# Where the high and low parts of a weight tile lie: two tensors, or one with the two parts value by value in turn

## The chip, the cores and the metric

The kernel runs on one core of a Trainium2 chip. The time is the device time of one execution in microseconds (us), from the first to the last of what the device does for it. The core has a matrix engine (TensorE, in the rows PE for the matmuls and PEld for the loads of the operand that is held in the array), a vector engine (VectorE, DVE), a scalar engine (ScalarE, ACT), a general engine (GpSimd, POOL) and a queue engine (SyncE, SP) that issues most DMAs. Each has its own list of instructions; they wait for one another by semaphores. Data lie in an on-chip memory of 128 partitions; matmul results go to eight banks of an accumulator memory.

## The reference

A stack of two layers on 256 tokens of width 1024, in float32. Each layer has a mixer (six mLSTM heads, five neighbourhood attention heads, five GLA heads in both directions), a cross-attention into 256 memory tokens, and a gated feed-forward block with a depthwise convolution. What matters here are the large products with weights:

```python
proj = h @ w_in                       # 1024 x 3512, cut into 13 parts
mixed @ w_out                         # 1024 x 1024
q = h @ wq; k = mem_n @ wk; v = mem_n @ wv; o @ wo
u = h @ w_up                          # 1024 x 5632
a, g = u[..., :D_FF], u[..., D_FF:]
a = dwconv_centred(a, conv_w, conv_b)
(jax.nn.gelu(a) * g) @ w_down         # 2816 x 1024
```

## The kernel before, in words

**Products in three passes.** A float32 matrix is split into a high part, which is the value rounded to the matmul's narrower format (float32r), and a low part, the rest. A product W x is then W_hi x_hi + W_hi x_lo + W_lo x_hi, all added up in one bank.

**Units.** The weights come in 144 units of at most 1 MB (128 partitions by up to 2048 float32), in the order that `UNITS` lists. Three slots (`RING` = 3) hold them. For each unit:
- SyncE issues the load into `raw` (line 573), once VectorE is done with the unit that was in that slot three before.
- ScalarE copies raw to the high part, `whi` (line 1108, in `hi_upto`), once the data have landed and the matmuls of the unit three before are done.
- VectorE writes raw minus high to the low part, `wlo` (line 1462, in `lo_upto`).
- TensorE waits for that (`have`) and runs the unit's matmuls, taking its operands from `weights`.

**Two kinds of unit.** In a feature-major unit (made by `fm`, with `KT` = 8 blocks of 128 input features, up to 256 output columns) the weights are the operand that is held in the array, 128 by 128 at a time, and the tokens stream through. They are used in `fm_blocks` (for each block three matmuls of 256 columns, the high weights against the high and the low tokens and the low weights against the high: lines 685 to 687 with a token tile xhi, xlo, chi or clo as the moving operand) and in `fm_joint` (line 723: high weights against the high and low tokens together, 512 columns; line 724: low weights against the high tokens, 256 columns). The gate and up projections of the FFN, the queries and keys of the cross-attention and nine units of each input projection are of this kind: 78 of 144. In the others (made by `tm`, 4 blocks, and the FFN's down projection, 2 blocks) a token tile is held, and the weights stream through as the moving operand, in up to 512 columns.

In the rows, `bank<-xhi,whi` names first the moving operand and then the held one.

**What sets the order.** Each engine's list is written out by hand; ScalarE and VectorE run the splits of later units between other work, at the places where `split_hi` and `split_lo` stand. In the FFN a group `p` uses three units: fa (gate), fg (up) and the down unit of the group before.

Of the kernel before, what the change touches and what calls it, by code (L numbers as in the profile page):

```python
# [15 lines left out]
F32R = mybir.dt.float32r  # L16
ALU = mybir.AluOpType
ACT = mybir.ActivationFunctionType
# [3 lines left out]
P = 128  # L22
# [4 lines left out]
TT, KT = T // P, DM // P  # L27
# [18 lines left out]
def layer_units(l):  # L46

    u = []

    def fm(name, m, *columns, at=l):  # L50
        u.append(((at, name), m, 0, KT, columns))

    def tm(name, m, c, n, halves="ab"):
        for half in halves:
            u.append(((l, name + half), m, 4 * "ab".index(half), 4, ((c, n),)))

    fm("gq", "w_in", (C_GQ, P))
    fm("mix", "w_in", (C_G, 32), (C_GQ + P, 32), (C_GK + P, 32), (C_GA, 32))
    fm("qk0", "w_in", (0, 256))
    fm("nqk4", "w_in", (C_NQ + 256, DH), (C_NK + 256, DH))  # L60
    fm("qk1", "w_in", (256, 256))
    fm("qk2", "w_in", (512, 256))
    tm("v", "w_in", C_V, ML)
    fm("nq", "w_in", (C_NQ, 256))
    fm("nk", "w_in", (C_NK, 256))
    fm("gk", "w_in", (C_GK, P))
    tm("nv", "w_in", C_NV, NA)
    tm("gv", "w_in", C_GV, GV)
    tm("o", "w_in", C_O, ML)
    tm("gg", "w_in", C_GG, GV)  # L70
    for i in range(2 if l else 0, 4):
        fm(f"xk{i}", "w_xk", (256 * i, 256))
    tm("xv0", "w_xv", 0, 512)
    tm("xv1", "w_xv", 512, 512, "a")
    tm("wo0", "w_out", 0, 512)
    tm("wo1", "w_out", 512, 512)
    tm("xv1", "w_xv", 512, 512, "b")
    for i in range(4):
        fm(f"xq{i}", "w_xq", (256 * i, 256))
    tm("xw0", "w_xo", 0, 512)  # L80
    tm("xw1", "w_xo", 512, 512)
    if l + 1 < DEPTH:
        fm("xk0", "w_xk", (0, 256), at=l + 1)
    for p in range(NP):
        fm(f"fa{p}", "w_up", (256 * p, 256))
        fm(f"fg{p}", "w_up", (FF + 256 * p, 256))
        if p:
            u.append(((l, f"fd{p - 1}"), "w_down", 2 * p - 2, 2, ((0, DM),)))
    u.append(((l, f"fd{NP - 1}"), "w_down", 2 * NP - 2, 2, ((0, DM),)))
    if l + 1 < DEPTH:  # L90
        fm("xk1", "w_xk", (256, 256), at=l + 1)
    return u

UNITS = [u for l in range(DEPTH) for u in layer_units(l)]
# [3 lines left out]
SIZE = [nk * w for (_, _, _, nk, _), w in zip(UNITS, WCOLS)]  # L98
RING = 3
UW = 2048  # L100
# [198 lines left out]
def build(nc, a, out):  # L299
    with ExitStack() as ctx:  # L300
        def sb(name, shape, dt=F32):
            return ctx.enter_context(nc.sbuf_tensor(name, shape, dt))

        def sem(name):
            return ctx.enter_context(nc.semaphore(name))
# [1 line left out]

        sb("to_line", [P, LINE // 4 - 48])
        raw = sb("raw", [P, RING, UW])
        whi = sb("whi", [P, RING, UW], F32R)  # L310
        wlo = sb("wlo", [P, RING, UW], F32R)

        h = sb("h", [P, TT, DM])
        tmb = sb("tmb", [P, TT, DM])
# [62 lines left out]
        rt = sb("rt", [P, TT])  # L377
        eps = sb("eps", [P, 1])
        gbias = sb("gbias", [24, 1])
        used = [0]  # L380

        def carve(*shape, at=None):
# [68 lines left out]
        hi_done = sem("hi_done")  # L451
        lo_done = sem("lo_done")
# [73 lines left out]
        def is_used(eng, l, unit):  # L526
            eng.wait_ge(te_done, USED[l, unit])
# [140 lines left out]
        def _(pe):  # L668
# [3 lines left out]
            for l in range(DEPTH):  # L672
# [15 lines left out]

                def weights(key, nk):
                    gu = UNIT[key]  # L690
                    return tuple(w[:, gu % RING, 0:SIZE[gu]].rearrange("p (k n) -> p k n", k=nk) for w in (whi, wlo))

                def fm_blocks(name, group, blocks, fresh=False, at=l):

                    u = at, name
                    if blocks[0][:2] == (0, 0):
                        free(name, at)
                    have(u)
                    hi, lo = weights(u, KT)
                    x = PAIR[group]  # L700
                    for f, k0, k1 in blocks:
                        for k in range(k0, k1):
                            if fresh and f == 0:
                                lo_is(pe, l, group, k)
                            cs = slice(f * P, f * P + P)
                            last = split_mm(bank_of(at, name, 2, T)[:, f, :], hi[:, k, cs], lo[:, k, cs], x[0][:, k, :], x[1][:, k, :],
                                            k == 0 and (f == 0 or k1 == KT), k == KT - 1)
                    if blocks[-1][2] == KT and blocks[-1][0] == WCOLS[UNIT[u]] // P - 1:
                        last.then_inc(te_done, 1)

                def fm_joint(name, fresh):

                    u = l, name
                    have(u)
                    hi, lo = weights(u, KT)
                    for f in range(2):
                        free(f"{name}{f}")
                        o = bank(f"{name}{f}")
                        for k in range(KT):
                            if fresh and f == 0:  # L720
                                lo_is(pe, l, "n2" if name[:2] == "xq" else "n3", k)
                            cs = slice(f * P, f * P + P)
                            mm(o, hi[:, k, cs], ypair[:, k].rearrange("p a n -> p (a n)"), start=k == 0, stop=False, skip_group_check=True)  # L723
                            last = mm(o[:, 0:T], lo[:, k, cs], yhi[:, k, :], start=False, stop=k == KT - 1, skip_group_check=True)  # L724
                        last.then_inc(te_done, 1)
# [4 lines left out]
                def tm_half(unit, half, names, n, group, fresh=False, tokens=(0, 1), ks=range(4)):  # L730
                    have((l, unit + half))
                    hi, lo = weights((l, unit + half), 4)
                    x = PAIR[group]
                    for t in tokens:
                        if half == "a":
                            free(names[t])
                        for k in ks:
                            kk = 4 * "ab".index(half) + k
                            if fresh and t == 0:
                                lo_is(pe, l, group, kk)  # L740
                            s = slice(t * P, t * P + P)
                            last = split_mm(bank(names[t])[:, 0:n], x[0][:, kk, s], x[1][:, kk, s],
                                            hi[:, k, :], lo[:, k, :], kk == 0, kk == KT - 1)
                        if (half == "b" or t == TT - 1) and k == 3:
                            last.then_inc(te_done, 1)
# [76 lines left out]
                if l == 0:  # L822
                    pe.wait_ge(memn_ready, TT)
                    for i in range(4):
                        free(f"mt_{i}")
                        for kk in range(2):
                            for t in range(TT):
                                k = 2 * i + kk
# [12 lines left out]
                for hh in range(MLH + 1):  # L841
# [7 lines left out]
                    if hh:  # L849
# [3 lines left out]
                        w = PT[:, g % 2, :]  # L853
# [194 lines left out]
                for p in range(NP + 1):  # L1048
# [3 lines left out]
                    if p:  # L1052
# [4 lines left out]
                        hi, lo = weights(u, 2)  # L1057
                        for i in (0, 2, 1, 3):
                            n, t = i // 2, i % 2
# [12 lines left out]
        def _(act):  # L1072
            A = nc.scalar.activation
# [28 lines left out]
            def hi_upto(l, unit):  # L1102
                while nhi[0] <= UNIT[l, unit]:
                    gu = nhi[0]
                    act.wait_ge(landed[gu % RING], 16 * LANDS[gu])
                    if gu >= RING:
                        is_used(act, *UNITS[gu - RING][0])
                    A(whi[:, gu % RING, 0:SIZE[gu]], raw[:, gu % RING, 0:SIZE[gu]], ACT.Copy).then_inc(hi_done, 1)  # L1108
                    nhi[0] += 1

            act.wait_ge(const_ready, 1)
# [6 lines left out]
            for l in range(DEPTH):  # L1118
# [5 lines left out]
                def split_hi(unit):  # L1124
                    hi_upto(l, unit)
# [250 lines left out]
                if l + 1 < DEPTH:  # L1376
                    hi_upto(l + 1, "xk0")
# [30 lines left out]
                if l + 1 < DEPTH:  # L1408
                    hi_upto(l + 1, "xk1")
# [14 lines left out]
        def _(dve):  # L1424
            V = nc.vector
            ts, tt, stt = V.tensor_scalar, V.tensor_tensor, V.scalar_tensor_tensor
# [30 lines left out]
            def lo_upto(l, unit):  # L1457
                while nlo[0] <= UNIT[l, unit]:
                    gu = nlo[0]
                    dve.wait_ge(hi_done, gu + 1)  # L1460
                    n_ = SIZE[gu]
                    tt(wlo[:, gu % RING, 0:n_], raw[:, gu % RING, 0:n_], whi[:, gu % RING, 0:n_], ALU.subtract).then_inc(lo_done, 1)  # L1462
                    nlo[0] += 1

            for l in range(DEPTH):
# [5 lines left out]
                def split_lo(unit):  # L1471
                    lo_upto(l, unit)
# [92 lines left out]
                for hh in range(MLH):  # L1565
                    is_filled(dve, l, f"mlb{hh}")
                    nb = bank(f"mlb{hh}", 2, T)
                    e, w = E[:, hh % 2, :], PT[:, hh % 2, :]
# [201 lines left out]
                if l + 1 < DEPTH:  # L1770
                    lo_upto(l + 1, "xk0")
# [32 lines left out]
                if l + 1 < DEPTH:  # L1804
                    lo_upto(l + 1, "gq")
# [4 lines left out]
                for i in (0, 2, 1, 3):  # L1810
                    n, t = i // 2, i % 2
# [46 lines left out]
```

## Time and profile before

| | us |
|---|---|
| median of three runs (lowest, highest) | 899.81 (896.81, 899.89) |
| the profiled execution's own time | 897.88 |
| its span, first to last instruction | 896.0 |
| TensorE busy with matmuls | 876.3 |
| TensorE's weight loads, beside them | 771.3 |
| VectorE busy | 626.8 |
| ScalarE busy | 525.2 |
| mean granted TensorE clock | 0.996 |

Matmuls overlap in the array and their ends are modelled, so a single matmul's busy time is longer than the distance between two starts. The distance of starts is what a stream costs. The busy time of a weight load also holds a fixed part. Durations of VectorE and ScalarE are those of one instruction after another.

### The profile page before, as it was taken

How to read it: one execution, taken by the hardware profiler on the slowest of the kernel's cores; microseconds unless marked ns; L12 is line 12 of the kernel's file. 1: busy time of each engine (PE TensorE's matmuls, PEld its weight loads, DVE VectorE, ACT ScalarE, POOL GpSimd, SP SyncE). 2: the span in 40 equal slices, each digit the busy share in tenths (PEclk: the TensorE clock that was granted, in tenths of full speed). 3: DMA queues.
4: the chain of work that ended last, by engine and by line, in shares of the span. 5: the costliest groups of instructions: out<-in, count | busy, mean ns of one | idle time of the engine just before them, and what ended most of it. 6: DMA issues, size and time to landing. Idle time of an engine off the chain costs nothing.

```text
span 896.0 us, 13415 instructions
## 1 busy us (share of the span) xinstructions
PE 876.3 (98%) x5453; PEld 771.3 (86%) x5453; DVE 626.8 (70%) x915; ACT 525.2 (59%) x782; POOL 15.3 (2%) x37
## 2 busy tenths in 40 slices
PE   6999999999999999999999999999999899999997
PEld 5999998888888888888899999888888788888885
DVE  5787588758557767667667975877664677667665
ACT  6954673647547556556576546735645655555555
POOL 5000000000000000000000000000000000000000
PEclk9999999999999999999999999999999999999999
DMA  9745453265154655555558254425352356565541
GB/s 280 219 113 157 166 164 121 97 232 188 48 188 157 219 188 188 188 189 187 141 150 231 80 161 165 142 95 188 140 189 95 128 177 212 188 196 180 189 165 47
DMA packets 128680, 146.68 MB, mean 164 GB/s; under 512 B 23165, under 2 KB 109547, under 8 KB 128619
## 3 DMA queue, kind: packets, MB, share of 16 engines
q1 hardware_dynamic: 128404, 145.55, 50.5%
q8 instruction: 43, 0.70, 0.3%
q10 hardware_dynamic: 214, 0.28, 0.1%
q14 instruction: 19, 0.15, 0.0%
HBM read 144.77 MB, written 1.05 MB: 163 GB/s over the span
## 4 chain that ended last, share of the span: by engine, by line
PE 91%; DVE 4%; ACT 3%; issue 1%; DMA 1%; SPq 1%; POOL 0%; DVEq 0%; ACTq 0%; POOLq 0%
PE bank L723 21%; PE bank L685 15%; PE bank L687 15%; PE bank L686 15%; PE bank L724 11%; PE bank L758 2%; PE bank L859 2%; PE bank L1030 2%; PE bank L1017 2%; DVE wlo L1462 2%; ACT whi L1108 1%; PE bank L891 1%; PE bank L868 1%; PE bank L777 1%; DMA raw<-in_w_in 1%
## 5 line engine op out<-in xcount | busy, mean ns | idle before, releaser
L1462 DVE TENSOR_TENSOR wlo<-raw,whi 128x2048 fp32r<-128x2048 f32 (+3 forms) x144 | 306.1, 2134 | 93.5 <-ACT whi L1108 92.9
L723 PE MATMUL bank<-ypair,whi 128*128 128x512 f32 x832 | 294.9, 398 | 0.6 <-DVE ypair L1478 0.5
L1108 ACT ACTIVATE whi<-raw 128x2048 fp32r<-128x2048 f32 (+3 forms) x144 | 256.5, 1787 | 36.6 <-PE bank L687 28.9
L724 PE MATMUL bank<-ypair,wlo 128*128 128x256 f32 x832 | 233.4, 280 | 0.0
L723 PEld LDWEIGHTS bank<-ypair,whi 128*128 128x128 f32 x832 | 156.2, 188 | 40.4 <-DVE wlo L1462 1.4
L724 PEld LDWEIGHTS bank<-ypair,wlo 128*128 128x128 f32 x832 | 157.1, 189 | 0.8
L685 PE MATMUL bank<-xhi,whi 128*128 128x256 f32 x320 | 93.7, 293 | 1.1 <-DVE wlo L1462 0.9
L686 PE MATMUL bank<-xlo,whi 128*128 128x256 f32 x320 | 91.2, 285 | 0.0
L687 PE MATMUL bank<-xhi,wlo 128*128 128x256 f32 x320 | 91.2, 285 | 0.0
L685 PE MATMUL bank<-whi,xhi 128*128 128x512 f32 (+2 forms) x256 | 90.1, 352 | 0.0
L687 PE MATMUL bank<-whi,xlo 128*128 128x512 f32 (+2 forms) x256 | 88.5, 346 | 0.0
L686 PE MATMUL bank<-wlo,xhi 128*128 128x512 f32 (+2 forms) x256 | 88.4, 345 | 0.0
L685 PE MATMUL bank<-whi,fhi 128*128 128x512 f32 x176 | 69.1, 393 | 0.0
L687 PE MATMUL bank<-whi,flo 128*128 128x512 f32 x176 | 68.8, 391 | 0.0
L686 PE MATMUL bank<-wlo,fhi 128*128 128x512 f32 x176 | 68.6, 390 | 0.0
L685 PEld LDWEIGHTS bank<-xhi,whi 128*128 128x128 f32 x320 | 62.1, 194 | 5.7 <-issue 4.1
L686 PEld LDWEIGHTS bank<-xlo,whi 128*128 128x128 f32 x320 | 62.2, 194 | 0.0
L687 PEld LDWEIGHTS bank<-xhi,wlo 128*128 128x128 f32 x320 | 62.1, 194 | 0.0
L685 PEld LDWEIGHTS bank<-whi,xhi 128*128 128x128 f32 x256 | 48.1, 188 | 5.1 <-issue 1.3
L687 PEld LDWEIGHTS bank<-whi,xlo 128*128 128x128 f32 x256 | 48.1, 188 | 3.8
L686 PEld LDWEIGHTS bank<-wlo,xhi 128*128 128x128 f32 x256 | 48.1, 188 | 3.5
L1392 ACT ACTIVATE arena<-bank 128x256 f32<-128x256 f32 x44 | 16.3, 380 | 57.4 <-PE bank L724 57.4
(264 smaller groups left out, 1194.0 us busy)
## 6 DMA issues: line engine op xcount, KB each, us to landing
raw<-in_w_up SPq DMA_DIRECT2D x44, 1024.0 KB, 5.0
raw<-in_w_down SPq DMA_DIRECT2D x22, 1024.0 KB, 5.0
raw<-in_w_in SPq DMA_DIRECT2D x10, 1024.0 KB, 6.2
raw<-in_w_xk SPq DMA_DIRECT2D x8, 1024.0 KB, 4.8
raw<-in_w_xv SPq DMA_DIRECT2D x8, 1024.0 KB, 4.9
raw<-in_w_out SPq DMA_DIRECT2D x8, 1024.0 KB, 4.9
raw<-in_w_xq SPq DMA_DIRECT2D x8, 1024.0 KB, 5.6
raw<-in_w_xo SPq DMA_DIRECT2D x8, 1024.0 KB, 5.0
```

Source lines behind the costliest of these rows:

```text
L685: mm(o, s_hi, m_hi, start=first, stop=False, skip_group_check=True)
L686: mm(o, s_hi, m_lo, start=False, stop=False, skip_group_check=True)
L687: return mm(o, s_lo, m_hi, start=False, stop=last, skip_group_check=True)
L723: mm(o, hi[:, k, cs], ypair[:, k].rearrange("p a n -> p (a n)"), start=k == 0, stop=False, skip_group_check=True)
L724: last = mm(o[:, 0:T], lo[:, k, cs], yhi[:, k, :], start=False, stop=k == KT - 1, skip_group_check=True)
L758: last = mm(bank(names[t])[:, 0:n], x[:, k, t * P:(t + 1) * P], w[:, k, :], start=k + i == 0, stop=False, skip_group_check=True)
L859: last = mm(o[:, t, d, :], w[:, c:c + P], mv[:, jt, g, :], start=i == 0, stop=i == len(src) - 1)
L1017: last = mm(bank(f"xs{hh}", TT, T)[:, t, :], xq[:, 2 * hh + kk, t * P:(t + 1) * P], xk[:, 2 * hh + kk, :], start=kk == 0, stop=kk == 1)
L1030: last = mm(bank(f"xo_{hh}", 2, T)[:, f, :], xv[:, jt, hh * XD + f * P:hh * XD + (f + 1) * P], xpt[:, hh, jt, :], start=jt == 0, stop=jt == 1)
L1108: A(whi[:, gu % RING, 0:SIZE[gu]], raw[:, gu % RING, 0:SIZE[gu]], ACT.Copy).then_inc(hi_done, 1)
L1392: A(fx[:, f, :], bank(f"fa{p}{f}")[:, T:2 * T], ACT.Copy).then_inc(fa_copied, 1)
L1462: tt(wlo[:, gu % RING, 0:n_], raw[:, gu % RING, 0:n_], whi[:, gu % RING, 0:n_], ALU.subtract).then_inc(lo_done, 1)
```

## The change

The tensors `whi` and `wlo`, each 128 partitions by 3 slots by 2048, become one tensor `whl`, 128 by 3 by 4096: as many bytes, in the same place. A new helper, `parts`, gives the two parts of a unit. For a feature-major unit (8 blocks) the slot holds high and low values in turn, high value 0, low value 0, high value 1, low value 1, and so on, and each part is a view with a step of two values, which is 8 bytes. For the other units the high part is the first half of the slot and the low part begins at its middle; each is contiguous, as before. ScalarE's copy, VectorE's subtraction and TensorE's operands take these views. `raw`, the transfers, the semaphores and the order of instructions on every engine are the same.

```diff
-        whi = sb("whi", [P, RING, UW], F32R)
-        wlo = sb("wlo", [P, RING, UW], F32R)
+        whl = sb("whl", [P, RING, 2 * UW], F32R)
...
+        def parts(gu):
+
+            w, n = whl[:, gu % RING, :], SIZE[gu]
+            if UNITS[gu][3] == KT:
+                v = w[:, 0:2 * n].rearrange("p (n a) -> p a n", a=2)
+                return v[:, 0, :], v[:, 1, :]
+            return w[:, 0:n], w[:, UW:UW + n]
+
...
                 def weights(key, nk):
                     gu = UNIT[key]
-                    return tuple(w[:, gu % RING, 0:SIZE[gu]].rearrange("p (k n) -> p k n", k=nk) for w in (whi, wlo))
+                    return tuple(w.rearrange("p (k n) -> p k n", k=nk) for w in parts(gu))
...
-                    A(whi[:, gu % RING, 0:SIZE[gu]], raw[:, gu % RING, 0:SIZE[gu]], ACT.Copy).then_inc(hi_done, 1)
+                    A(parts(gu)[0], raw[:, gu % RING, 0:SIZE[gu]], ACT.Copy).then_inc(hi_done, 1)
...
-                    n_ = SIZE[gu]
-                    tt(wlo[:, gu % RING, 0:n_], raw[:, gu % RING, 0:n_], whi[:, gu % RING, 0:n_], ALU.subtract).then_inc(lo_done, 1)
+                    hi, lo = parts(gu)
+                    tt(lo, raw[:, gu % RING, 0:SIZE[gu]], hi, ALU.subtract).then_inc(lo_done, 1)
```

## Rows read from the trace of the kernel before

**Rows 1.** Busy time of each engine, from the page.
```profile
PE 876.3 (98%) x5453; PEld 771.3 (86%) x5453; DVE 626.8 (70%) x915; ACT 525.2 (59%) x782; POOL 15.3 (2%) x37
```

**Rows 2.** The chain that ended last, from the page: share by engine.
```profile
PE 91%; DVE 4%; ACT 3%; issue 1%; DMA 1%; SPq 1%; POOL 0%; DVEq 0%; ACTq 0%; POOLq 0%
```

**Rows 3.** Costliest groups: line, engine, out<-in, count | busy, mean ns | idle before.
```profile
L723 PE MATMUL bank<-ypair,whi 128*128 128x512 f32 x832 | 294.9, 398 | 0.6 <-DVE ypair L1478 0.5
...
L724 PE MATMUL bank<-ypair,wlo 128*128 128x256 f32 x832 | 233.4, 280 | 0.0
L723 PEld LDWEIGHTS bank<-ypair,whi 128*128 128x128 f32 x832 | 156.2, 188 | 40.4 <-DVE wlo L1462 1.4
...
L685 PE MATMUL bank<-xhi,whi 128*128 128x256 f32 x320 | 93.7, 293 | 1.1 <-DVE wlo L1462 0.9
...
L685 PEld LDWEIGHTS bank<-xhi,whi 128*128 128x128 f32 x320 | 62.1, 194 | 5.7 <-issue 4.1
```

**Rows 4.** Timeline of TensorE in a 256-column stream: start us, duration us, instruction.
```profile
502.30 0.28 PE L686 MATMUL bank<-xlo,whi 128*128 128x256 f32 x1
...
503.01 0.28 PE L686 MATMUL bank<-xlo,whi 128*128 128x256 f32 x1
```

**Rows 5.** Timeline of TensorE in a joint stream of the FFN.
```profile
364.66 0.40 PE L723 MATMUL bank<-ypair,whi 128*128 128x512 f32 x1
364.90 0.28 PE L724 MATMUL bank<-ypair,wlo 128*128 128x256 f32 x1
365.02 0.40 PE L723 MATMUL bank<-ypair,whi 128*128 128x512 f32 x1
...
367.84 0.40 PE L723 MATMUL bank<-ypair,whi 128*128 128x512 f32 x1
```

**Rows 6.** Timeline of the weight loads, after a wait.
```profile
710.37 0.19 PEld L723 LDWEIGHTS bank<-ypair,whi 128*128 128x128 f32 x1 [0.31 <-DVE wlo L1462]
710.48 0.19 PEld L724 LDWEIGHTS bank<-ypair,wlo 128*128 128x128 f32 x1
```

**Rows 7.** Groups of instructions by form: the two splits, 2048 values.
```profile
L1462 DVE TENSOR_TENSOR wlo<-raw,whi 128x2048 fp32r<-128x2048 f32 x116 | 265.0, 2290 | 89.7 <-ACT whi L1108 89.3
...
L1108 ACT ACTIVATE whi<-raw 128x2048 fp32r<-128x2048 f32 x116 | 221.2, 1911 | 34.0 <-PE bank L687 28.9 <-PE bank L758 4.5 <-DMA raw<-in_w_in 0.4
```

**Rows 8.** Single lines: min/median/max ns, first and last start us, forms.
```profile
L1646 DVE SCALAR_TENSOR_TENSOR den<-arena x2: 194/194/195, 106.8 to 554.6; 128x24 f32<-128x24 f32 x2
...
L1590 DVE SCALAR_TENSOR_TENSOR arena<-arena,tmb x2: 1218/1218/1218, 59.2 to 507.7; 128x1024 f32<-128x1024 f32 x2
...
L1711 DVE SCALAR_TENSOR_TENSOR gg<-eg,gg x2: 817/819/821, 159.7 to 598.0; 128x640 f32<-128x640 f32 x2
```

**Rows 9.** Busy time by engine in one group of the FFN: window, length, us.
```profile
358.40:375.20 16.80, 16.80 (x90) 14.32 (x89) 11.55 (x14) 9.31 (x11) 0.00 (x0) 1.00 0.57 188
```

**Rows 10.** Timeline of VectorE in the FFN.
```profile
362.82 2.29 DVE L1462 TENSOR_TENSOR wlo<-raw,whi 128x2048 fp32r<-128x2048 f32 x1 [1.11 <-ACT whi L1108]
```

**Rows 11.** Timeline of TensorE where the next unit's stream begins.
```profile
369.61 0.40 PE L723 MATMUL bank<-ypair,whi 128*128 128x512 f32 x1
```

**Rows 12.** The chain in order of time, where the splits stand in it.
```profile
14.51 1.92 ACT whi L1108
16.46 2.30 DVE wlo L1462
...
202.71 1.81 ACT whi L1108
204.54 2.30 DVE wlo L1462
...
554.74 1.81 ACT whi L1108
556.64 2.29 DVE wlo L1462
...
641.09 1.81 ACT whi L1108
642.92 2.30 DVE wlo L1462
```

**Rows 13.** Timeline of TensorE in another joint stream.
```profile
721.92 0.39 PE L723 MATMUL bank<-ypair,whi 128*128 128x512 f32 x1
...
723.31 0.39 PE L723 MATMUL bank<-ypair,whi 128*128 128x512 f32 x1
```

## The prediction

> **What bounds the kernel now.** I read the busy times first. TensorE is busy for 876.3 of 896.0 us, its weight loads for 771.3 us beside that, VectorE for 626.8 and ScalarE for 525.2 us [rows 1]. The chain of waits says the same: 91% of the span runs over TensorE, 4% over VectorE, 3% over ScalarE [rows 2]. So a change counts in two ways only: it alters the pace of the matmul stream, or it makes one of the few waits for weights longer. The costliest groups come next [rows 3]. The matmuls that hold a weight tile in the array are L723 and L724 (832 of each) and the L685, L686 and L687 that stream xhi or xlo (320 of each, and 32 of each with chi and clo). These have their stationary operand, a 128x128 piece of whi or wlo, loaded once for every matmul. The others stream whi and wlo and hold a token tile; their units keep the old layout.
>
> Busy times of single matmuls say little about pace, since they overlap. I take the pace from starts in the timeline. In a stream of 256-column matmuls, starts are 0.118 us apart (502.30 to 503.01, six steps) [rows 4]. In the joint stream of L723 (512 columns) and L724 (256), nine pairs take 3.18 us (364.66 to 367.84), 0.353 us a pair; of a pair, 0.24 us go by under the 512 columns and 0.11 to 0.12 us under the 256 [rows 5]. How fast a weight load can follow another is seen where the array was empty: after a wait, two loads start at 710.37 and 710.48, 0.11 us apart [rows 6]. So under a 256-column matmul the load fits with some 0.01 us to spare, and under a 512-column one with more than 0.1 us.
>
> **The change, part by part.** No instruction, wait, transfer or semaphore is added, removed or moved; three kinds of operand get a step.
>
> (a) Weight loads, 2 x 832 + 3 x 352 = 2720 of them, read 128 values with a step of 8 bytes instead of 4. The trace has no load with that step, so I bound it. Now a load walks through 512 bytes of a partition in 0.11 us, 4.7 bytes per ns. With the step it walks through 1024. If it goes on at 4.7 bytes per ns, it takes 0.22 us; if only the count of values matters, 0.11 us as now; less than now is possible only if the load were not paced by its 128 values, for which no row speaks. The nearest row is the moving operand of the same engine: L723's 512 columns are 2048 bytes, walked in 0.24 us at most [rows 5], 8.5 bytes per ns or more. At that pace the 1024 bytes take 0.12 us at the most. I take 0.11 us: cost nothing. The cover is thin: every ns by which a load outgrows the slot costs 832 + 1056 = 1888 ns, 1.9 us, because the loads that lie under 256 columns are those for L723 (832) and those for the 1056 short matmuls. The 832 loads for L724 lie under 512 columns.
>
> The Trainium skill (SBUF — State Buffer, Door 1, the box on cachelines) says that the memory has lines of 16 bytes and that two accesses to a line are enough for full bandwidth. A step of 8 bytes gives just two, so by that rule the sum is that of no change. No row of this case shows a line.
>
> (b) ScalarE's copy that writes the high part (L1108), 1.91 us for 2048 values, and (c) VectorE's subtraction that reads it and writes the low part (L1462), 2.29 us [rows 7]. Of the 144 units, 78 are of the changed kind (70 of them with 2048 values). The nearest row for a step on VectorE is L1646, which reads two operands of 24 values with a step of 260 bytes: 194 ns. The same kind of instruction without a step is L1590, 1218 ns for 1024 values, and L1711, 819 for 640 [rows 8]: (1218 - 819) / 384 = 1.04 ns a value and 153 ns fixed, so 24 values would be 178 ns. The step of 260 bytes cost 16 ns, 0.7 ns a value. For a step of 8 bytes that is the upper end, 1.4 us for 2048 values; the lower is zero. I know no row for a step in ScalarE's writes; I give it the same two ends. I take zero for both, because 260 bytes puts each value far from the last and 8 bytes does not, but this is a guess between two ends and I keep the upper one as a rival.
>
> Even the upper end would mostly be hidden. A group of the FFN lasts 16.8 us, in which VectorE works 11.55 and ScalarE 9.31 us [rows 9]; two changed units add 2.9 us to each. The subtractions end long before their use: the one that ends at 365.11 (362.82 + 2.29) [rows 10] is for the weights whose stream begins at 369.61 [rows 11], 4.5 us later. The places with no cover are those where copy and subtraction stand in the chain of waits: four such pairs of changed units, at 14.51, 202.71, 554.74 and 641.09 us [rows 12]. There the cost would be 4 x 2 x 1.4 = 11 us.
>
> **The sum** against the profiled execution's own 897.9 us (span 896.0): 0 + 0 + 0. The median of the three runs is 899.8, 1.9 us above the profiled one, and the comparison is made with such runs, so the forecast is 900.
>
> **Rivals.** (A) The strided load is paced by bytes, not values. Slower: a load of 0.22 us and the 0.01 us by which a short slot now exceeds its load give 0.23 us where 0.118 stands. 1056 x 0.11 = 116 us in the L685 to L687 streams and 832 x 0.11 = 92 us in the joint ones: 897.9 + 208 = 1106 us. It decides from the point where a load needs more than the 0.118 us of a slot; a load of 0.123 us would already cost about 9 us. For it speaks that the margin is 0.01 us and that weight loads are the one stream that must cover twice the ground; against it, that the same engine already moves through memory at that pace for its other operand.
>
> (B) The step slows VectorE and ScalarE as 260 bytes did. TensorE keeps its pace, the hidden part stays hidden, and the four uncovered places cost 11 us: 911 us. For it: 16 ns of L1646. Against: the step there is over 32 times as long. The Trainium skill (Vector Engine (DVE) Microarchitecture Reference, 5.2 Measured stream behaviour on trn2) speaks for it: a port keeps its rate only with pairs of adjacent words, and values one by one cost 1.7 to 2.5 ns each. By its highest figure a subtraction would take 3 us more, and two of them in a group would lift VectorE to 17.5 of 16.8 us; it would then bind in the FFN. L1646 agrees in size (1.04 + 0.7 ns a value); the page has no figure for a step of 8 bytes.
>
> (C) The pace changes by itself. The joint stream knows two rhythms: 0.353 us a pair in rows 5, but four pairs in 1.39 us, 0.3475 a pair, elsewhere [rows 13], at the same granted clock and with the same instructions. If the new loads tipped all of it into the quicker one, 832 x 0.0058 = 4.8 us would go: 895 us. Nothing in the change points to it, and the slower rhythm is already the usual one, so it can hardly get worse by this.
>
> **Chances.** No change 0.65; A (in full or by some ns a load) 0.14; B 0.13; C 0.08. What a measurement of this kernel can tell from no change is about 0.5%, 4.5 us; the three runs lie within 3.1 us. Faster by more than that: C, 0.08, and 0.01 for what I did not think of. Slower: A and B together, 0.27. Within: 0.64. The range of 8 in 10 reaches down to C and up over B, 894 to 912; A in full is left out.
>
> **What would show it.** Right: starts in the 256-column streams 0.118 us apart, joint pairs at 0.3475 to 0.353 us, L1108 and L1462 at 1.91 and 2.29 us as a mean of the 2048 forms. A shows as short matmuls 0.13 to 0.23 us apart and weight loads longer than their 188 to 194 ns [rows 3], while the streams of whi and wlo keep their pace. B shows as L1462 of 2048 values above 2.3 us and L1108 above 1.9, and TensorE waits on L1462 at the four places. C shows as pairs at 0.3475 us throughout. I would be wrong if the load pays for its step by only a few ns, which no view of the old kernel can exclude.

## The result and the profile after

The changed kernel takes 902.13 us (median of 20 runs, 899.23 to 904.69), the kernel before 899.92 in the same measurement. The ratio is 1.0025, 95% interval 1.0014 to 1.0035. A repeat beside other kernels gave 1.0027 (1.0012 to 1.0041). So the step of 8 bytes costs about a quarter of a per cent, 2.2 us: less than the 0.5% that I called a change, but a real loss and not zero. Its profiled execution has a span of 899.9 us.

The page answers to [rows 1] with VectorE as it was, 2 us more of matmuls, 10 us more of ScalarE and 9 us more of weight loads:

```profile
PE 878.2 (98%) x5453; PEld 779.9 (87%) x5453; DVE 625.9 (70%) x915; ACT 535.6 (60%) x782; POOL 14.9 (2%) x37
```

Where they come from is in the groups by form (busy us, mean ns), which answer to [rows 3, 7]. The helpers moved the lines by seven: L1469 is the subtraction, L1115 the copy, L730 and L731 the joint stream.

```profile
L1469 DVE TENSOR_TENSOR whl<-raw,whl 128x2048 fp32r<-128x2048 f32 x116 | 265.1, 2291 | 94.9 <-ACT whl L1115 94.8
L1115 ACT ACTIVATE whl<-raw 128x2048 fp32r<-128x2048 f32 x116 | 233.4, 2017 | 29.9 <-PE bank L694 25.3 <-PE bank L765 4.4
L731 PEld LDWEIGHTS bank<-ypair,whl 128*128 128x128 f32 x832 | 163.7, 197 | 0.7
L730 PEld LDWEIGHTS bank<-ypair,whl 128*128 128x128 f32 x832 | 162.7, 196 | 34.4 <-DVE whl L1469 2.0 <-issue 0.7
```

The subtraction reads one operand and writes the other with the step, and costs nothing more: 2291 against 2290 ns. The copy went from 1911 to 2017 ns on the mean of 116. Only 70 of them are of the changed kind, and those went from 1911 to 2085 ns, 0.17 us more each. A weight load of the joint stream records 196 or 197 ns instead of 188.

Does the longer load slow the stream? The starts of TensorE, against [rows 4] and [rows 5]:

```profile
503.09 0.28 PE L693 MATMUL bank<-xlo,whl 128*128 128x256 f32 x1
...
503.81 0.28 PE L693 MATMUL bank<-xlo,whl 128*128 128x256 f32 x1
...
366.24 0.40 PE L730 MATMUL bank<-ypair,whl 128*128 128x512 f32 x1
...
369.42 0.40 PE L730 MATMUL bank<-ypair,whl 128*128 128x512 f32 x1
```

Six steps of the short stream take 0.72 us, 0.120 each, and nine joint pairs 3.18 us, 0.353 each. Taken over all such steps, the median of the short streams is 120 ns in both traces. The joint pairs go from 354.0 to 355.6 ns on the mean, which contains the longer waits, and from 350 to 354 on the median. The loads after a wait, where nothing else is in the array, answer to [rows 6]:

```profile
714.53 0.19 PEld L730 LDWEIGHTS bank<-ypair,whl 128*128 128x128 f32 x1 [0.45 <-DVE whl L1469]
714.64 0.20 PEld L731 LDWEIGHTS bank<-ypair,whl 128*128 128x128 f32 x1
```

To the nanosecond, such pairs of loads start 108 or 109 ns apart before and 114 to 117 ns apart now. The slot under a 256-column matmul is 120 ns. It just holds. And the wait itself, 0.31 us before [rows 6], is 0.45 us: this is where the change is paid.

Both traces have the same 5453 matmuls in the same order, so each step from one start to the next can be compared. There are exactly eight places at which the step is longer, by 0.14 us or more, in the changed kernel and stays so in every trace with strided copies, and not in the traces below with copies of the old length. With the start before and the growth: 111.65 us (0.15), 206.89 (0.18), 274.58 (0.17), 458.70 (0.25), 466.96 (0.18), 559.47 (0.16), 645.27 (0.18), 710.37 (0.16). Together 1.4 us. Two of the places, before and after:

```profile
206.88 0.19 PEld L723 LDWEIGHTS bank<-ypair,whi 128*128 128x128 f32 x1 [0.37 <-DVE wlo L1462]
458.69 0.86 PEld L777 LDWEIGHTS bank<-ident,tmb 128*128 128x128 f32 x8 [0.19 <-DVE tmb L1453]
```
```profile
207.30 0.19 PEld L730 LDWEIGHTS bank<-ypair,whl 128*128 128x128 f32 x1 [0.54 <-DVE whl L1469]
459.69 0.85 PEld L784 LDWEIGHTS bank<-ident,tmb 128*128 128x128 f32 x8 [0.44 <-DVE tmb L1460]
```

Four of the eight waits (206.89, 274.58, 645.27, 710.37) end with a subtraction. The one at 458.70 ends with `tmb`, a normalised tile that VectorE writes after a subtraction: the longer copy delays what stands behind it in the engines' lists too. For the other three the profile names no releaser. In the chain of the kernel before, five of the eight waits are not seen as such. They are put down as part of a matmul, as the one at 710.37, where the usual step is 0.24 us:

```profile
710.39 0.47 PE bank L723
```

The rest of the profiled difference of 3.9 us is TensorE's clock. In the windows (length, then busy us, then granted clock, DMA share, GB/s) the kernel before has a stretch at the lower level, 1.2 GHz, in the first and the changed one in the second:

```profile
476.00:484.00 8.00, 8.00 (x44) 6.99 (x43) 4.93 (x6) 6.62 (x9) 0.00 (x0) 0.79 0.73 149
584.00:592.00 8.00, 8.00 (x93) 6.53 (x88) 7.75 (x22) 0.52 (x1) 0.00 (x0) 1.00 0.35 109
```
```profile
476.00:484.00 8.00, 8.00 (x55) 6.80 (x54) 4.51 (x8) 5.58 (x8) 0.00 (x0) 1.00 0.77 182
584.00:592.00 8.00, 8.00 (x104) 6.29 (x101) 6.26 (x17) 1.20 (x1) 0.00 (x0) 0.57 0.23 69
```

From 575 to 600 us the changed kernel takes 3.1 us longer. Its gain near 480 us is 1.5 us, of which 0.8 goes to a longer wait that follows at 502 us. So 1.4 + 3.1 - 0.7 = 3.8 of the 3.9 us are accounted for.

### The profile page after: what moved, and what is told of

Same layout as the page of the kernel before. It is cut to its first block, busy times and chain, and to the rows that moved or that the text cites. A ratio compares the mean times of both kernels' runs of the same rounds, so it can differ in the third digit from the quotient of the medians.

```text
span 899.9 us, 13415 instructions
## 1 busy us (share of the span) xinstructions
PE 878.2 (98%) x5453; PEld 779.9 (87%) x5453; DVE 625.9 (70%) x915; ACT 535.6 (60%) x782; POOL 14.9 (2%) x37
## 3 DMA queue, kind: packets, MB, share of 16 engines
HBM read 144.77 MB, written 1.05 MB: 162 GB/s over the span
## 4 chain that ended last, share of the span: by engine, by line
PE 83%; DVE 7%; ACT 7%; issue 1%; DMA 0%; DVEq 0%; ACTq 0%
PE bank L730 20%; PE bank L692 13%; PE bank L693 13%; PE bank L694 13%; PE bank L731 10%; DVE whl L1469 3%; ACT whl L1115 3%; PE bank L765 2%; PE bank L866 2%; PE bank L1037 2%; PE bank L1024 2%; ACT ypair L1139 1%; PE bank L898 1%; PE bank L784 1%; DVE ypair L1727 1%
## 5 line engine op out<-in xcount | busy, mean ns | idle before, releaser
L1469 DVE TENSOR_TENSOR whl<-raw,whl 128x2048 fp32r<-128x2048 f32 (+3 forms) x144 | 306.2, 2135 | 99.0 <-ACT whl L1115 98.6
L730 PE MATMUL bank<-ypair,whl 128*128 128x512 f32 x832 | 295.4, 398 | 1.3 <-DVE whl L1469 0.6
L1115 ACT ACTIVATE whl<-raw 128x2048 fp32r<-128x2048 f32 (+3 forms) x144 | 269.4, 1877 | 32.5 <-PE bank L694 25.3
L731 PE MATMUL bank<-ypair,whl 128*128 128x256 f32 x832 | 232.8, 280 | 0.0
L730 PEld LDWEIGHTS bank<-ypair,whl 128*128 128x128 f32 x832 | 162.7, 196 | 34.4 <-DVE whl L1469 2.0
L731 PEld LDWEIGHTS bank<-ypair,whl 128*128 128x128 f32 x832 | 163.7, 197 | 0.7
L692 PE MATMUL bank<-xhi,whl 128*128 128x256 f32 x320 | 92.9, 290 | 2.3 <-DVE whl L1469 1.7
L692 PE MATMUL bank<-whl,xhi 128*128 128x512 f32 (+2 forms) x256 | 90.6, 354 | 0.0
L694 PE MATMUL bank<-xhi,whl 128*128 128x256 f32 x320 | 90.4, 283 | 0.0
L693 PE MATMUL bank<-whl,xhi 128*128 128x512 f32 (+2 forms) x256 | 88.7, 346 | 0.0
L693 PE MATMUL bank<-whl,fhi 128*128 128x512 f32 x176 | 68.7, 390 | 0.0
L692 PE MATMUL bank<-whl,fhi 128*128 128x512 f32 x176 | 68.7, 390 | 0.0
L692 PEld LDWEIGHTS bank<-xhi,whl 128*128 128x128 f32 x320 | 62.5, 195 | 6.9 <-issue 5.6
L694 PEld LDWEIGHTS bank<-xhi,whl 128*128 128x128 f32 x320 | 62.5, 195 | 0.0
L692 PEld LDWEIGHTS bank<-whl,xhi 128*128 128x128 f32 x256 | 48.3, 189 | 5.3 <-issue 1.5
L693 PEld LDWEIGHTS bank<-whl,xhi 128*128 128x128 f32 x256 | 48.4, 189 | 3.5
```

What stands on the lines that cost most here:

```text
L692: mm(o, s_hi, m_hi, start=first, stop=False, skip_group_check=True)
L693: mm(o, s_hi, m_lo, start=False, stop=False, skip_group_check=True)
L694: return mm(o, s_lo, m_hi, start=False, stop=last, skip_group_check=True)
L1115: A(parts(gu)[0], raw[:, gu % RING, 0:SIZE[gu]], ACT.Copy).then_inc(hi_done, 1)
L1469: tt(lo, raw[:, gu % RING, 0:SIZE[gu]], hi, ALU.subtract).then_inc(lo_done, 1)
```

## The experiments

**The two halves of the change, and the one tensor alone.** The first kernel has contiguous writes and reads the held operand with the step, the second the reverse, the third neither. `writes(gu)` and `Held` stand for `parts(gu)` on the two sides.

```diff
-A(parts(gu)[0], raw[:, gu % RING, 0:SIZE[gu]], ACT.Copy)
+A(hi, r, ACT.Copy)        # r, hi, lo = writes(gu): halves in held_step8, step 2 in written_step8
...
-tuple(w.rearrange("p (k n) -> p k n", k=nk) for w in parts(gu))
+Held(gu, 0), Held(gu, 1)  # step 2 in held_step8, halves in written_step8
```

> Only TensorE's held operand is read with a step of 8 bytes; ScalarE and VectorE write contiguous halves, so the held values are the right ones in a wrong order, and the output is not the reference's. Theory 1 (the load pays a little): the weight loads of changed units last 0.196 us as in the changed kernel, joint pairs stand 0.3548 us apart instead of 0.3533, and the time is 1 to 1.5 us above before (ratio 1.001 to 1.002); the copy of 2048 values is back at 1.91 us. Theory 2 (only the writes pay): loads at 0.188 us, ratio 1.000. Theory 3 (the one tensor in place of two costs, not the step): as the changed kernel, 1.0025, in this run and in all of this set.

> Only ScalarE's copy and VectorE's subtraction use the step of 8 bytes; TensorE reads contiguous halves, so values are in a wrong order and the output is not the reference's. Theory 1: the copy lasts 2.05 to 2.09 us where before it lasted 1.90, the subtraction 2.29 as before, loads 0.188 us; the time is about 1 us above before (ratio 1.001), from the handful of places where a copy stands in the chain, 0.15 us each. Theory 2 (only the writes pay): ratio 1.0025. In both the subtraction is unchanged.

> The one tensor for both parts, but contiguous halves everywhere, no step. Theories 1 and 2: copy 1.91, subtraction 2.29, load 0.188 us, ratio 1.000 within 0.001. Theory 3: ratio 1.0025.

Measured: held_step8 0.999 (0.9974 to 1.0006), written_step8 1.0005 (0.9995 to 1.0016), one_tensor 0.9997 (0.9983 to 1.0012). Loads, copies and subtractions were as theory 1 has them:

```profile
L1148 ACT ACTIVATE whl<-raw 128x2048 fp32r<-128x2048 f32 x116 | 221.3, 1912 | 33.9 <-PE bank L724 28.3 <-PE bank L797 4.5 <-DMA raw<-in_w_in 0.9
L762 PEld LDWEIGHTS bank<-ypair,whl 128*128 128x128 f32 x832 | 162.7, 196 | 33.5 <-DVE whl L1502 1.3
```
```profile
L1148 ACT ACTIVATE whl<-raw 128x2048 fp32r<-128x2048 f32 x116 | 233.0, 2013 | 30.8 <-PE bank L724 26.0 <-PE bank L797 4.5 <-DMA raw<-in_w_in 0.2
L762 PEld LDWEIGHTS bank<-ypair,whl 128*128 128x128 f32 x832 | 156.3, 188 | 41.2 <-DVE whl L1502 2.0
```

The first fence is held_step8, the second written_step8. Theory 3 is out: one tensor costs nothing. Of theory 1, the part that the longer loads cost 1 to 1.5 us fell: held_step8 shows nothing. In the traces the eight steps named above grew by 1.4 us in written_step8 and by 0.0 in held_step8 and in one_tensor, each in sum. The median joint pair is 354 ns in held_step8 too, against 350 in written_step8 and one_tensor, but its mean is 354.3, as in one_tensor (354.4): the longer load changes the rhythm of the joint stream and not its pace. The medians of the runs alone would not have carried this; a microsecond is at their limit, and the two halves, 0.999 and 1.0005, do not add up to 1.0025. The comparison at equal clock below settles it.

> The changed kernel once more, beside the others, because its 1.0025 and the 0.999 and 1.0005 of its halves do not add up within the medians. Theory 1 (the parts add): 1.000 to 1.002, copy 2.05 to 2.09 us for a changed unit of 2048 values. Theory 2 (reading and writing with the step disturb each other): again 1.0025 or more, with loads or copies longer than in the halves.

Measured 1.0027 (1.0012 to 1.0041), so the change costs what it cost, and nothing in its trace disturbs anything else: copy 2017 ns, loads 196 and 197 ns, the same eight steps longer by 1.4 us in sum. It had the low clock at 586 to 594 us too (0.57), which the three kernels above had not.

**Is it the copy's length?** In the first kernel the units that TensorE waits for keep contiguous halves. The second and third are the kernel before with nothing strided and a longer way to each copy.

```diff
# old_at_waits
+OLD = ("gq", "mix", "qk0", "xk0", "xk1", "xk2", "xk3", "xq0", "xq1", "xq2", "xq3", "fa0", "fg0", "fa1")
-            if UNITS[gu][3] == KT:
+            if UNITS[gu][3] == KT and UNITS[gu][0][1] not in OLD:
# copy_plus1, copy_plus3
+if UNITS[gu][3] == KT:
+    for _ in range(1):    # or 3
+        A(extra[:, at_extra[0]:at_extra[0] + 1], eps[:, :], ACT.Copy)
```

> The changed kernel, complete, but the units whose copy stands at a wait of TensorE (gq, mix, qk0, the keys and queries of the cross-attention, and the first three of each FFN) keep contiguous halves; the other feature-major units, 40 of the 44 FFN projections among them, keep the step of 8 bytes. Theory 1 (ten waits, each longer by the 0.16 us that a strided copy takes more, make the difference): 1.000 to 1.001, and in the trace the streams after the waits are back at their length of before. Theory 2 (the step costs pace in the streams themselves): about 1.002, since four fifths of the strided loads are still there.

> The kernel before, complete and without any step, with one more ScalarE activation of a single value ahead of the copy of each feature-major unit, about 0.2 us each. Theory 1: the same ten waits grow by 0.2 us each: 1.002 to 1.003, as in the changed kernel. Theory 2 (the step, not the copy's length): 1.000.

> As copy_plus1 with three such activations, about 0.6 us: theory 1: three times as much, 1.006 to 1.008, unless waits that had cover begin to show as well. Theory 2: 1.000.

Measured: old_at_waits 1.0000 (0.9984 to 1.0015), copy_plus1 0.9998 (0.9986 to 1.0009), copy_plus3 1.0036 (1.0020 to 1.0052). The first is as theory 1 says: with 50 of the 78 strided units still there, 38 of the 44 gate and up projections among them (not 40, as I wrote), the loss is gone. The sizes of the other two were expected too large, because I took an activation's 0.197 us for its delay. The next one starts 92 ns after it, so the delays were 0.09 and 0.28 us. In copy_plus3, three of them and the copy behind them:

```profile
448.39 0.37 ACT L1112 ACTIVATE extra<-eps 128x1 f32<-128x1 f32 x3
448.67 1.90 ACT L1114 ACTIVATE whi<-raw 128x2048 fp32r<-128x2048 f32 x1
```

The same wait as above, in old_at_waits, copy_plus1 and copy_plus3:

```profile
710.10 0.19 PEld L732 LDWEIGHTS bank<-ypair,whl 128*128 128x128 f32 x1 [0.36 <-DVE whl L1471]
```
```profile
712.63 0.19 PEld L725 LDWEIGHTS bank<-ypair,whi 128*128 128x128 f32 x1 [0.39 <-DVE wlo L1468]
```
```profile
713.38 0.19 PEld L725 LDWEIGHTS bank<-ypair,whi 128*128 128x128 f32 x1 [0.58 <-DVE wlo L1468]
```

0.31 us without delay, 0.39 with 0.09 and 0.58 with 0.28: the wait grows by the delay, one for one, and 0.45 with the strided copy's 0.17 lies on the same line. This one wait scatters by 0.05 us where nothing delays it, 0.36 in old_at_waits and 0.27 in held_step8. The other places agree: seven of the eight steps grew by 0.09 to 0.11 us each in copy_plus1 and by 0.27 to 0.29 in copy_plus3. The one at 458.70 grew by 0.18 and 0.56, twice as much.

**The whole runs, at equal clock.** TensorE's mean granted clock differs from run to run, and with it the time, by more than the change costs. Beside these experiments the kernel before ran 72 times, each with its clock on record: the 21 runs at 0.996 or more took 896.8 to 899.0 us, the other 51 took 898.4 to 903.0. I compared only runs at 0.996 or more; this split was made after the runs.

| kernel | such runs | mean, us | over the kernel before | growth at the eight places, us |
|---|---|---|---|---|
| before | 21 | 898.0 | | |
| changed, both measurements | 7 | 899.8 | 1.8 | 1.4 |
| held_step8 | 7 | 897.8 | -0.3 | 0.0 |
| written_step8 | 9 | 899.8 | 1.8 | 1.4 |
| one_tensor | 4 | 898.0 | 0.0 | 0.0 |
| old_at_waits | 5 | 897.5 | -0.6 | 0.1 |
| copy_plus1 | 7 | 899.0 | 1.0 | 0.9 |
| copy_plus3 | 3 | 900.6 | 2.6 | 2.5 |

The strided writes alone cost what the whole change costs, the strided loads cost nothing, and a delay of the copy costs its sum over the eight places. Copy_plus1 does show its expected microsecond here. The kernels in which no copy is late at these places scatter by up to 0.6 us, so the 0.4 us between 1.8 and 1.4 is within the scatter.

**Larger steps.** With 16 bytes, a slot has four lanes, two for each part; with 32, eight. In step12 only the eight units of 1024 values have the larger step.

```diff
-v = w[:, 0:2 * n].rearrange("p (n a) -> p a n", a=2)
+v = w[:, 0:2 * n].rearrange("p (n a) -> p a n", a=4)   # 8 for step32
...
+m = 2                                                 # high part v[:, 0:m], low part v[:, m:2 * m]
```

> The step is doubled to 16 bytes everywhere: in a changed unit two of four lanes hold the high part and two the low part; the computation is complete. Theory A (every 16 bytes passed cost one access, which carries at most one value now): a load needs twice its time, 0.22 us between two loads instead of 0.11, short slots 0.12 to about 0.23 us, 1888 slots times 0.11 = 208 us, so about 1108 us; copy and subtraction of 2048 values go to 3.5 to 4 us. Theory B (only the count of values sets the pace, whatever the step): 902 us, all durations as in the changed kernel. Theory C (bytes walked set the pace, and 8 bytes was just below the limit): loads 0.2 us or more as in A, but copy and subtraction grow in proportion from their own limits.

> 32 bytes everywhere; the computation is complete. Theory of 16-byte accesses: at 16 bytes each value already costs an access of its own, so nothing changes: about 1162 us, copy 3.95, subtraction 3.9 us, short streams 234 ns. Rival (the distance counts, as in bytes walked): loads and splits double again, short streams 0.43 us, the time over 1600 us. Rival 2 (values share some wider line of 32 or 64 bytes at 16 bytes of step): slower than 1162 but by less than double.

> The changed kernel, complete, but the eight units of 1024 values have a step of 12 bytes (the third value of three is unused); all others 8 bytes. If each 16 bytes entered cost 1.83 ns, as 8 and 16 bytes of step suggest (three steps of four enter new 16 bytes at 12), a value costs 1.37 ns: copy of 1024 values about 0.2 + 1.40 = 1.6 us (contiguous 1.04, step 8 1.13), subtraction 0.15 + 1.41 = 1.56 us (1.22 contiguous). If instead every step that is no longer below half of 16 bytes costs a full access, 2.1 and 2.0 us, as with 16 bytes. The time stays within 0.5% of the changed kernel.

Measured 1162.05, 1189.73 and 911.76 us. Groups of step16 (first fence), step12 (second) and step32 (third):

```profile
L1502 DVE TENSOR_TENSOR whl<-raw,whl 128x2048 fp32r<-128x2048 f32 x116 | 377.3, 3276 | 184.2 <-ACT whl L1148 184.1
L1148 ACT ACTIVATE whl<-raw 128x2048 fp32r<-128x2048 f32 x116 | 359.8, 3141 | 9.3 <-PE bank L724 6.0 <-PE bank L797 3.1
```
```profile
L1154 ACT ACTIVATE whl<-raw 128x1024 fp32r<-128x1024 f32 x8 | 13.0, 1621 | 2.0 <-DMA raw<-in_w_in 1.9
L1508 DVE TENSOR_TENSOR whl<-raw,whl 128x1024 fp32r<-128x1024 f32 x8 | 12.8, 1599 | 4.0 <-ACT whl L1154 4.0
```
```profile
L1502 DVE TENSOR_TENSOR whl<-raw,whl 128x2048 fp32r<-128x2048 f32 x116 | 389.1, 3379 | 194.3 <-ACT whl L1148 194.2
L1148 ACT ACTIVATE whl<-raw 128x2048 fp32r<-128x2048 f32 x116 | 372.2, 3249 | 9.3 <-PE bank L724 6.0 <-PE bank L797 3.1
```

The contiguous forms of 1280 values in the kernel before are:

```profile
L1462 DVE TENSOR_TENSOR wlo<-raw,whi 128x1280 fp32r<-128x1280 f32 x12 | 17.7, 1485 | 0.6 <-ACT whi L1108 0.6
L1108 ACT ACTIVATE whi<-raw 128x1280 fp32r<-128x1280 f32 x12 | 15.2, 1266 | 0.0
```

With the fixed part taken off (ScalarE 191 ns, VectorE 143, each from the contiguous forms of 2048 and 1280 values) and the means resolved to the changed units:

| step | ScalarE, ns a value | VectorE | load, ns a value |
|---|---|---|---|
| contiguous | 0.84 | 1.05 | 0.85 |
| 8 bytes | 0.92 | 1.05 | 0.91 |
| 12 bytes | 1.40 | 1.42 | 1.37 |
| 16 bytes | 1.83 | 1.85 | 1.82 |
| 32 bytes | 1.92 | 1.93 | 1.89 |

ScalarE's writes, VectorE's operands and the weight loads, whose contiguous rates differ, meet at nearly one price: about 1.84 ns for each new 16 bytes of a partition that an operand enters. A value enters a half of one at a step of 8, three quarters at 12, one at 16 and above. For ScalarE and VectorE this fits: half the price is 0.92 ns, over ScalarE's own 0.84, so it pays a little at 8 bytes, and under VectorE's 1.05, which pays nothing. For the loads the column mixes two measures. The first two entries are from pairs of loads after a wait (108 to 109 and 114 to 117 ns). The other three are the pace of short streams (here step12, step16 and step32, in this order), which at 8 bytes is set by the matmul and not by the load:

```profile
16.64 0.34 PE L729 MATMUL bank<-xlo,whl 128*128 128x256 f32 x1
...
18.91 0.34 PE L730 MATMUL bank<-xhi,whl 128*128 128x256 f32 x1
```
```profile
59.87 0.40 PE L724 MATMUL bank<-xhi,whl 128*128 128x256 f32 x1
...
61.97 0.40 PE L724 MATMUL bank<-xhi,whl 128*128 128x256 f32 x1
```
```profile
58.81 0.40 PE L724 MATMUL bank<-xhi,whl 128*128 128x256 f32 x1
...
65.84 0.40 PE L723 MATMUL bank<-xlo,whl 128*128 128x256 f32 x1
```

Thirteen steps in 2.27 us, nine in 2.10 and 29 in 7.03: 0.175, 0.233 and 0.242 us. After a wait, two loads with a step of 16 bytes start less far apart, as here in held_step16:

```profile
874.73 0.31 PEld L762 LDWEIGHTS bank<-ypair,whl 128*128 128x128 f32 x1 [0.27 <-issue]
874.94 0.33 PEld L763 LDWEIGHTS bank<-ypair,whl 128*128 128x128 f32 x1
```

Such pairs are 211 to 214 ns apart, 1.66 ns a value. Half of that is 0.83, under the contiguous 0.85. So that the load's 0.91 at 8 bytes is half a price and not something else is not shown.

Of the theories given, the one by count of values and the one by bytes walked fall. The durations are those of A and of the 16-byte one, but A's time of 1108 us was missed by 54 us, and the 16-byte one said that nothing changes from 16 to 32 bytes. The 28 us between them are the last few per cent of the table, not a doubling; the rule does not give them, and rival 2 (slower, by less than double) allows for them. Their cause is open. In step12, 192 loads that need 55 ns more than their slot make 10.6 us; measured are 10 us over the changed kernel, outside the 0.5% that I had allowed because I had not priced the loads.

**Which side of the 262 us?**

> Only the held operand is read with a step of 16 bytes, the writes are contiguous; wrong order of values, the output is not the reference's. From the run with 16 bytes everywhere: 234 ns from start to start in the short streams instead of 120, a joint pair 0.47 us instead of 0.353: 1056 x 0.114 + 832 x 0.117 = 218 us, so 1116 us if the splits stay covered, and 1162 if the loads alone make all of the 262 us.

> Only copy and subtraction use a step of 16 bytes; TensorE reads contiguous halves; wrong order of values, the output is not the reference's. Theory 1: the copy of a changed unit takes 3.95 and the subtraction 3.9 us, 2.0 and 1.6 us more than contiguous; covered in the FFN (VectorE 11.55 + 3.2 of 16.8 us), so only the uncovered places pay, 4 to 12 of them times 3.6 us: 915 to 945 us. Rival: the FFN's chain from projection to activation is in the way and each of 22 groups pays up to 1 us more: 965 us. Loads stay at 0.188 us.

Measured 1108.37 and 1068.48 us. The held operand alone costs 209 us, near the sum of the slots, 1056 x 0.113 + 832 x 0.114 = 214 us. The writes alone cost 169 us where I expected 15 to 65. The timeline of VectorE and ScalarE in one FFN group of written_step16 says why:

```profile
405.79 0.63 ACT L1446 ACTIVATE fhi<-arena 128x512 fp32r<-128x512 f32 x1 [4.43 <-DVE arena L1841]
406.33 5.66 ACT L1148 ACTIVATE whl<-raw 128x2048 fp32r<-128x2048 f32 x2
...
417.75 3.89 ACT L1148 ACTIVATE whl<-raw 128x2048 fp32r<-128x2048 f32 x1
...
427.03 0.63 ACT L1446 ACTIVATE fhi<-arena 128x512 fp32r<-128x512 f32 x1 [4.44 <-DVE arena L1841]
```
```profile
410.31 6.07 DVE L1502 TENSOR_TENSOR whl<-raw,whl 128x2048 fp32r<-128x2048 f32 x2 [3.16 <-ACT whl L1148]
...
421.68 3.87 DVE L1502 TENSOR_TENSOR whl<-raw,whl 128x2048 fp32r<-128x2048 f32 x1 [2.00 <-ACT whl L1148]
```

Neither engine is full, but each waits for the other in turn: copies, subtractions, convolution, copy, subtraction, gate product, next group. In their written order these form one chain of 21.2 us from one L1446 to the next, longer than the 16.8 us of TensorE's group. TensorE's weight loads wait up to 4.7 us for L1502 (in total, times, longest us), and its clock falls as well (0.942 over the run, against 0.996):

```profile
PEld bank L762 <- DVE whl L1502: 84.7, 29, 4.7
```

With 16 bytes on both sides the prices, 209 and 169 us, give only 262 together. The FFN group shows why. Its median length is 16.8 us in the kernel before, 20.4 in held_step16, 21.3 in written_step16 and 21.4 in step16: the longer of TensorE's group and the chain sets it, not their sum.

## Why the prediction was right, and where it was not

- **The forecast** of no change by the 0.5% bound, 900 us, stands; the loss of 2.2 us is inside the range. I had put the cost of all three parts at zero, and one of them was not. That the loads cost nothing was in part luck: the slot ends 3 ns above what they need.
- **(a) Loads.** The interval was 0.11 to 0.22 us, I took the lower end, it is 0.116. The slot of 0.118 to 0.120 us covers it with 3 ns to spare, so "the cover is thin" was truer than I knew: at 12 bytes it is gone. My reason, that the moving operand walks memory as fast, led to the right end but is not the mechanism. The price is mostly by 16 bytes entered. The Trainium skill's rule (SBUF — State Buffer, Door 1, the box on cachelines), lines of 16 bytes and full bandwidth from two accesses to a line, agrees with the traces in kind: a step of 8 bytes is nearly free, one of 16 is not. "Full bandwidth" is 7 to 10% too kind for the loads and ScalarE, and what the box draws from it, that four float32 values can be stepped for free, does not hold here (1.84 ns a value).
- **Rival A** is false at 8 bytes. At 16 its number comes out, 1106 us against the 1108 of held_step16, but not its reason: paced by bytes, the short slots would double again at 32 bytes, and they went from 0.233 to 0.242 us.
- **(b) ScalarE's copy** is the step that failed, as a term mis-sized. I had zero, a guess between two ends; it is 0.17 us a unit, an eighth of my upper end, and written_step8 shows that this alone makes the loss (1.8 us at equal clock).
- **(c) VectorE's subtraction** cost zero, as I took it. The 0.7 ns a value of L1646 belong to steps of 16 bytes and more (0.8 ns at 16). The rule of the Trainium skill (Vector Engine (DVE) Microarchitecture Reference, 5.2 Measured stream behaviour on trn2), that only adjacent pairs keep the rate, does not hold at 8 bytes here: 2291 ns.
- **The uncovered places.** I read four from the chain of waits. Eight steps grew, and only three of my four are among them; the one at 14.51 us lies in the start, which scatters by up to 0.4 us between kernels. At the other five the chain stays on TensorE and puts the wait down as part of a matmul. With eight places and 0.17 us the sum is 1.4 us, as measured at the steps, and most of the 1.8 us at equal clock.
- **The cover in the FFN** was judged by busy time and by the distance from a subtraction's end to its use. At 8 bytes that was enough. It is no rule: written_step16 has VectorE busy for 14.4 of 21.2 us and is bound by the chain between two engines.
- **Rival C** did not come. The median pair went the other way, from 350 to 354 ns, at an unchanged pace in held_step8.
- **Open:** what TensorE's clock adds. A stretch at 1.2 GHz near 590 us was in both profiled executions of the changed kernel and in none of the kernel before, its halves, or the delays. Of the changed kernel's 32 runs, nine had a mean granted clock of 0.992 or less and took 902.5 to 904.7 us; of the 72 runs of the kernel before, four had. So the changed kernel seems to fall that low more often, though written_step8, with the same late copies, did not in any of its 12 runs. Since 1.8 us remain at equal clock, this is the smaller part of the 2.2; why it comes, no run shows.

## What to carry to other kernels

Count the new 16-byte pieces that an operand enters per value and hold that, at about 1.84 ns each, against the engine's own time for a value: for the three kinds of operand measured here, a step of 8 bytes in float32 is nearly free, 12 is not, 16 costs about double, and beyond that little more. For a layout of weights that are held in the array, compare the load with the shortest matmul above it, not with the mean. Price a longer producer by all the places where its consumer waits now, for it or for what stands behind it in its engine's list, and by the chain of alternating waits between two in-order engines, not by busy shares. And where the clock moves the time by more than the change does, compare runs of equal clock.

## What the runs showed of the hardware that was not expected

- ScalarE's writes, VectorE's operands and, in a stream, the weight loads share one price for scattered float32 values, 1.82 to 1.85 ns at 16 bytes, though their contiguous rates are 0.84, 1.05 and 0.85 ns.
- The loads' record grows with the step: in the joint stream 188 ns, 196 at 8 bytes and 310 to 334 at 16.
- A one-value activation records 0.197 us but holds up the next by 0.092 us.
